# The FFN's high and low inner activations as alternating words of one tile, in a two-layer hybrid decoder

## The reference

```python
D_MODEL, SEQ, DEPTH, D_FF = 1024, 256, 2, 2816

def swiglu(h, w_gate, w_up, w_down):
    return (jax.nn.silu(h @ w_gate) * (h @ w_up)) @ w_down

for l in range(DEPTH):
    h = rms_norm(x, ffn1_norm[l])
    x = x + 0.5 * swiglu(h, ffn1_w_gate[l], ffn1_w_up[l], ffn1_w_down[l])
    ...
    h = rms_norm(x, ffn2_norm[l])
    x = x + 0.5 * swiglu(h, ffn2_w_gate[l], ffn2_w_up[l], ffn2_w_down[l])
```

## Time and profile before

| | |
|---|---|
| median of 3 runs | 1030.73 us (1030.73 to 1031.29) |
| span of the profiled execution, first to last instruction | 1029.2 us |
| TensorE's mean granted clock, as a share of full speed | 0.998 |
| busy: TensorE matmuls, weight loads | 1018.1 us, 887.9 us |
| busy: VectorE, ScalarE, GpSimd | 738.5 us, 603.0 us, 210.0 us |
| read from HBM, over the span | 175.05 MB, 171 GB/s |

### The profile page before, as it was taken

The page is one execution under the profiler, slowest core; times in us unless marked ns, Lnnn a source line. Parts: engine busy times, 40 slices in busy tenths (PEclk is TensorE's granted clock), DMA queues, the critical chain, the costliest instruction groups (busy, mean ns, idle before and its releaser), DMA issues.

```text
span 1029.2 us, 19004 instructions
## 1 busy us (share of the span) xinstructions
PE 1018.1 (99%) x6482; PEld 887.9 (86%) x6482; DVE 738.5 (72%) x1204; ACT 603.0 (59%) x1101; POOL 210.0 (20%) x248
## 2 busy tenths in 40 slices
PE   9999999999999999999999999999999999999996
PEld 7888888899988888888888888889999888888885
DVE  6677666798776866666777666678986877666665
ACT  6555555776655655555675555558675575555554
POOL 2867111100400211111111111110014003111111
PEclk9999999999999999999999999999999999999999
DMA  7966666584124666666747666665732238666661
GB/s 246 281 201 188 185 192 190 138 247 153 63 63 123 192 197 187 193 190 184 205 136 211 184 184 188 192 171 164 226 103 66 88 95 266 185 189 196 184 184 41
DMA packets 249881, 176.79 MB, mean 172 GB/s; under 512 B 5875, under 2 KB 235400, under 8 KB 249704
## 3 DMA queue, kind: packets, MB, share of 16 engines
q1 hardware_dynamic: 248800, 174.35, 57.2%
q0 software_dynamic: 400, 1.43, 0.4%
q10 hardware_dynamic: 632, 0.34, 0.1%
HBM read 175.05 MB, written 1.05 MB: 171 GB/s over the span
## 4 chain that ended last, share of the span: by engine, by line
PE 95%; DVE 2%; ACT 2%; issue 0%; DVEq 0%; POOL 0%; POOLq 0%; ACTq 0%
PE bank L742 30%; PE bank L745 16%; PE bank L726 13%; PE bank L727 13%; PE bank L728 13%; PE bank L786 1%; PE bank L1138 1%; PE bank L1125 1%; PE bank L1061 1%; PE bank L751 1%; ACT big L1455 1%; DVE X L1894 1%; PE bank L793 1%; ACT X L1462 1%; DVE Wl L1852 0%; ACT L1567 0%
## 5 line engine op out<-in xcount | busy, mean ns | idle before, releaser
L1852 DVE TENSOR_TENSOR Wl<-raw,Wh 128x1024 fp32r<-128x1024 f32 x324 | 413.8, 1285 | 77.7 <-ACT Wh L1391 77.6
L1391 ACT ACTIVATE Wh<-raw 128x1024 fp32r<-128x1024 f32 x323 | 330.5, 1054 | 84.1 <-PE bank L728 82.2
L742 PE MATMUL bank<-X,Wh 128*128 128x512 f32 x1344 | 336.8, 393 | 0.0
L742 PEld LDWEIGHTS bank<-X,Wh 128*128 128x128 f32 x1344 | 246.8, 188 | 48.9
L745 PEld LDWEIGHTS bank<-X,Wl 128*128 128x128 f32 x1344 | 182.9, 189 | 14.3 <-DVE Wl L1852 0.3
L609 POOL TENSOR_TENSOR gact<-gact,pooled 128x256 f32<-128x256 f32 x85 | 73.8, 868 | 575.7 <-DVE gact L1951 567.1
L745 PE MATMUL bank<-X,Wl 128*128 128x256 f32 x1344 | 187.2, 282 | 0.0
L726 PE MATMUL bank<-Wh,aH 128*128 128x512 f32 x336 | 132.9, 395 | 0.0
L727 PE MATMUL bank<-Wl,aH 128*128 128x512 f32 x336 | 131.9, 392 | 0.0
L728 PE MATMUL bank<-Wh,aL 128*128 128x512 f32 x336 | 131.5, 391 | 0.0
L1506 ACT ACTIVATE dec<-bank 128x256 f32<-128x256 f32 x88 | 33.6, 382 | 118.6 <-PE bank L745 118.5
(11 more groups left out here) (319 smaller groups left out, 1291.7 us busy)
## 6 DMA issues: line engine op xcount, KB each, us to landing
raw<-in_ffn_w_gate SPq DMA_DIRECT2D x88, 512.0 KB, 3.8
raw<-in_ffn_w_up SPq DMA_DIRECT2D x88, 512.0 KB, 3.7
raw<-in_ffn_w_down SPq DMA_DIRECT2D x88, 512.0 KB, 4.3
raw<-in_w_in SPq DMA_DIRECT2D x48, 512.0 KB, 4.3
raw<-in_w_out SPq DMA_DIRECT2D x16, 512.0 KB, 3.5
cst<-in_consts POOLq DMA_DIRECT2D x1, 1200.0 KB, 6.2
xr<-in_x SPq DMA_DIRECT2D x2, 512.0 KB, 4.2
out_x<-big SPq DMA_DIRECT2D x3, 256.0 KB, 2.7
```

The source lines that it names most:

```text
L742: nc.tensor.matmul(b[:, :], piece(Wh, s)[:, k, :], X[:, k, :, :], start=k == 0, stop=False)
L1391: return nc.scalar.activation(Wh[:, s, 0:D_MODEL], raw[:, s, :], ACT.Copy).then_inc(hi_cast.sem, 1)
L1852: return nc.vector.tensor_tensor(Wl[:, s, 0:D_MODEL], raw[:, s, :], Wh[:, s, 0:D_MODEL].bitcast(F32), ALU.subtract).then_inc(lo_cast.sem, 1)
```

## The change

One tile `A` takes the place of `aH` and `aL`. Its last dimension has two words, the high part at the even and the low part at the odd places; `aH` and `aL` are views of it with a step of two words. All code that writes or reads them is as it was.

```diff
         gate_raw = sb("gate_raw", [P, DEPTH, KT, GATES])
-        aH = sb("aH", [P, 2, SEQ], F32R)
-        aL = sb("aL", [P, 2, SEQ], F32R)
+        A = sb("A", [P, 2, SEQ, 2], F32R)
+        aH, aL = A[:, :, :, 0], A[:, :, :, 1]
         gact = sb("gact", [P, 2, SEQ])
```

## The result

Sixteen runs of each kernel on one chip: the changed kernel takes 1033.53 us (median; 1032.76 to 1034.12), the kernel before 1031.23 us (1030.63 to 1032.10). The ratio is 1.0020 with a 95% interval of 1.0013 to 1.0028: 2.3 us slower, by about as much as the 0.2% that the prediction called "no change". The two sets of runs don't overlap, so the difference is real, and the time stands just inside the top of the range (1033.6).

What follows compares the result with a forecast made beforehand. It took TensorE, busy 99% of the span, as the bound. Span 1029.2 us + 0 for loads + 0.1 at FFN ends, with the timed median's 1.5 above the span kept, gave 1030.8; range from 1.4 us under the median to 1033.6.

Steps and rivals of the forecast that it cites:

- (a): 1056 weight loads reading aH or aL with the 8-byte step: no change taken, up to three times the reading part as bound.
- "same": Outcome within about 0.2% (2.1 us) of the kernel before, which counts as no change; chance 0.79.
- the case that was given 0.18: Outcome slower than the 0.2% a measurement can tell: 0.15 from slower weight loads plus 0.03 from the element-wise engines.
- element-wise rival: VectorE and ScalarE pay for single words; only the four FFN ends show it, 0 to 2.8 us, up to 1033.6; chance 0.11.
- Which row was taken as nearest: ScalarE's writes of line 1712, two words then a gap of two against runs of four: 0.29 and 0.28 us.
- The cover: Under a 512-column matmul 0.12 us is free to hide a longer load; under a 256-column one only some 0.01 us.
- load rival: Loads' 108 ns reading part stretches for single words; chance 0.11 up to double, 0.04 for more (1083, at the bound 1140).
- a doubled load: Reading part doubled: the 88 first loads under a 256-column matmul cost 8.6 us, the other 968 stay hidden; 1039.4.
- (b): ScalarE's write of aH, 418 ns at 256 columns: bounds 0 to +0.22 us, taken +0.01.
- (c): VectorE's read of aH and write of aL, 425 ns at 256 columns: bounds 0 to +0.54 us, taken +0.01.

## Why the prediction came out as it did

- **The forecast's number.** 1030.8 was given, 1033.53 measured, at the top of the range. The step that failed is the sum of (a), "1056 x 0 = 0". The load takes 6.5 ns more (195 against 188), and down's matmuls stand on average 1.1 ns further apart, 13.4 ns a tile. With the gate and up runs' 11.6 it makes 25.0 ns x 88 = 2.2 us. The measured ratio, 1.0020, lies at the bound between the forecast's "same" and the case that was given 0.18. The prediction's own sign of being wrong, "if TensorE's starts move anywhere in the loop", came true.
- **The range held by luck.** It reaches to 1033.6 only because of 2.8 us that the element-wise rival might cost at the four ends of the FFNs. Nothing was paid there; the 2.3 us came from the loads in the loop, whose cases the range left out, and that these cost less than 2.8 us was not foreseen.
- **Which row was taken as nearest.** A ScalarE write in pairs stood for a TensorE load of single words. It told nothing of TensorE, and for ScalarE itself it was low as well: +18 ns on 256 words, not +10.
- **The cover.** "Such a load may grow to about 2.1 times its length unseen" is wrong in the small. A load that ends well within its 230 ns still moves the starts: with a step of three its reading part is some 108 + 65 = 173 ns, an estimate, and down's matmuls behind the first two still start 3 ns further apart on average. In the change this is 13.4 ns x 88 = 1.2 us. How a load that ends in time moves a start isn't shown; that it is +30 ns in odd and -2 in even tiles says that it isn't a fixed rest of each load.
- **The load rival.** Its mechanism, the reading part that stretches for single words, is what happened; its place was not. It expected the price at the 88 first loads, from 10 ns on; at 6.5 ns more these cost nothing, as its own threshold said (from down's first matmul to its second, where the step of four pays, it is 230 ns against 231 before, and from the last 745 to the first 119 against 121). The price sits in the loads that it called hidden and in runs that load nothing stepped. For a doubled load, at a step of four, the first loads pay 118 ns each, 9.9 us in the 84 tiles whose loads have that step, near the 8.6 that it gave; the whole is 17.9 us, since down's other matmuls (+7 ns each) and gate and up pay too. There the reading part, by the same estimate 108 + 123 = 231 ns, just reaches the 230 ns of its cover.
- **Parts (b) and (c).** ScalarE pays 18 ns, inside its bounds; VectorE pays 1 ns where up to 540 was allowed. Both are hidden in the loop and, as the kernel with stepped writes alone shows, at the four ends of the FFNs as well (ratio 0.9999). The rule of the Trainium skill's Vector Engine (DVE) Microarchitecture Reference, Measured stream behaviour on trn2, that a port needs adjacent pairs for its full rate, doesn't hold for a step of two words here: 426 ns against 425.
- **No term at all** stood in the prediction for gate and up. That a stream of unchanged matmuls takes 9.8 ns a tile more, by what the loads in down before it are like, was not among the rivals.

## What to carry to other kernels

A step of 8 bytes in a matmul's stationary operand of 4-byte words is cheap and not free (0.2% here); 12 bytes cost 0.9%, and from 16 bytes on the load's reading time doubles, which cost 1.7% and 2.4% here even under 512-column matmuls. In the moving operand avoid gaps: there the same step halved TensorE's rate, and pairs with a gap of two did no better (longer runs weren't tried). And where TensorE bounds a kernel with thousands of matmuls, compare start-to-start distances by position between two traces: a mean tile of 8.35 us repeated to 0.2 and 1.0 ns between executions of the two kernels, and the comparison shows what no wait and no busy share does. Look at the single tiles as well as at the mean, since a loop over pairs can have two kinds.

## What the runs showed of the hardware that was not expected

- The moving side at half rate with a step of two, 453 ns for 512 words, though half of every 16 bytes is used, which is two words of a line. The Trainium skill's rule of two hits a line (Advanced Engine Details and Errata, Memory Cachelines) would have it at the full rate; here the measurement decides against it for this operand.
- Two rhythms of an unchanged stream of matmuls, by what ran before them: the same sixteen take 2780 or 2801 ns in the odd tiles, and 2806 in the even ones whatever the loads (2777 and 2816 with a step of eight). One stepped load of the twelve is enough to switch, and the eight of the high part alone don't.
- VectorE reads and writes every second word as fast as adjacent ones (426 ns for 256 against 425), while ScalarE's writes take 0.07 ns a word more (18 / 256).
